# Hybrid decoder trunk: forget logits by row products on VectorE, the first weight block in four pieces, and two operations moved ahead of the last eviction

## What is computed

```python
def token_mixer_block(x, w_in, ...):
    h = jnp.einsum('bsd,dn->bsn', x, w_in)          # n = 10 * 512 + 4
    (p_in, hq, hf, hi, hg, gu, gv, fq, fk, fv, ff) = jnp.split(h, splits, axis=-1)
    ...
    d = fox_mixer(fq, fk, fv, ff + b_fox_f)
    ...
    gates = jax.nn.sigmoid(jnp.einsum('bsd,dn->bsn', x, w_gate) + b_gate)

def reference(x, ...):
    for l in range(DEPTH):
        x = layer_norm(ALPHA * x + token_mixer_block(...), ln1_g[l], ln1_b[l])
        x = layer_norm(ALPHA * x + peer_ffn(...), ln2_g[l], ln2_b[l])
```

## Time and profile before

| | us |
|---|---|
| median of 3 runs | 3813.95 (3813.29 to 3815.09) |
| the profiled execution's own time | 3812.06 |
| its span, from first to last instruction | 3810.1 |
| TensorE matmul busy | 3728.1 (98% of the span) |
| VectorE busy | 2730.8 (72%) |
| ScalarE busy | 1487.8 (39%) |
| mean granted TensorE clock | 0.996 of full |

### The profile page before, as it was taken

The page is one execution under the profiler, slowest core; times in us unless marked ns, Lnnn a source line. Parts: engine busy times, 40 slices in busy tenths (PEclk is TensorE's granted clock), DMA queues, the critical chain, the costliest instruction groups (busy, mean ns, idle before and its releaser), DMA issues. The chain is left out here.

```text
span 3810.1 us, 53339 instructions
## 1 busy us (share of the span) xinstructions
PE 3728.1 (98%) x19506; PEld 3310.0 (87%) x19506; DVE 2730.8 (72%) x5347; ACT 1487.8 (39%) x2154; POOL 1284.5 (34%) x1040
## 2 busy tenths in 40 slices
PE   8999999999999999999999999999999999999998
PEld 7878888999999999988878788889999899999887
DVE  3257635499989888878642566355999888888887
ACT  2244522244763333333322445223447533333332
POOL 1000000265856555544000000002658556555440
PEclk9999999999999999999999999999999999999999
DMA  4212423254689999999732225233537899999995
GB/s 148 101 56 75 161 91 138 108 184 157 216 287 382 358 355 348 344 346 354 257 133 94 65 68 171 78 139 112 206 142 229 302 378 357 358 350 344 342 357 208
DMA packets 321524, 847.59 MB, mean 222 GB/s; under 512 B 21056, under 2 KB 119360, under 8 KB 296256
## 3 DMA queue, kind: packets, MB, share of 16 engines
q1 hardware_dynamic: 247616, 576.84, 42.9%
q0 software_dynamic: 73728, 268.47, 18.8%
HBM read 755.58 MB, written 89.65 MB: 222 GB/s over the span
## 5 line engine op out<-in xcount | busy, mean ns | idle before, releaser
L93 PE MATMUL bank<-xT_low,u_high 128*128 128x384 f32 (+1 forms) x2144 | 728.9, 340 | 11.5 <-ACT hid L1897 7.3
L95 PE MATMUL bank<-xT_high,u_low 128*128 128x384 f32 (+1 forms) x2144 | 723.4, 337 | 0.0
L94 PE MATMUL bank<-xT_high,u_high 128*128 128x384 f32 (+1 forms) x2144 | 723.1, 337 | 0.0
L93 PE MATMUL bank<-v_low,w_high 128*128 128x512 f32 x1536 | 597.7, 389 | 0.9 <-DVE v_low L1998 0.9
L95 PE MATMUL bank<-v_high,w_low 128*128 128x512 f32 x1536 | 598.2, 389 | 0.0
L94 PE MATMUL bank<-v_high,w_high 128*128 128x512 f32 x1536 | 598.1, 389 | 0.0
L1189 POOL TENSOR_TENSOR u_low<-merged,u_high 128x1024 fp32r<-128x1024 f32 x96 | 243.1, 2546 | 1043.8 <-ACT u_high L1184 1043.6
L1257 POOL DMA_INDIRECT far_rows<-peer_v_dram,far_index x256 | 389.3, 1521 | 415.3 <-DVE x_far L1281 369.5
L1257 POOL DMA_INDIRECT far_rows<-peer_u_rows_dram,far_index x256 | 374.8, 1464 | 312.6 <-DVE far_dots L1263 259.7
L1998 DVE TENSOR_TENSOR v_low<-v_raw,v_high 128x1024 fp32r<-128x1024 f32 x256 | 301.8, 1221 | 207.4 <-ACT v_high L1909 207.3
L1909 ACT ACTIVATE v_high<-v_raw 128x1024 fp32r<-128x1024 f32 x256 | 257.3, 1052 | 472.2 <-PE bank L95 467.2
(11 more groups left out here) (445 smaller groups left out, 6811.3 us busy)
## 6 DMA issues: line engine op xcount, KB each, us to landing
merged<-peer_u_dram SPq DMA_DIRECT2D x128, 1024.0 KB, 7.7
v_raw<-peer_v_dram SPq DMA_DIRECT2D x128, 1024.0 KB, 9.4
gates_scratch<-stage SPq DMA_DIRECT2D x24, 2048.0 KB, 8.3
G<-gates_scratch SPq DMA_DIRECT2D x64, 768.0 KB
hidden_scratch<-ahead_hid SPq DMA_DIRECT2D x60, 384.0 KB, 2.6
hid<-hidden_scratch SPq DMA_DIRECT2D x30, 768.0 KB, 7.1
mg_raw<-w_merge_dram SPq DMA_DIRECT2D x28, 768.0 KB, 4.3
first_raw<-w_in_dram SPq DMA_DIRECT2D x20, 1024.0 KB, 5.6
```

Of the source, the lines that this page charges most:

```text
L93: nc.tensor.matmul(out, lh, rl, start=first, stop=False)
L94: nc.tensor.matmul(out, lh, rh, start=False, stop=False)
L95: return nc.tensor.matmul(out, ll, rh, start=False, stop=last)
```

## The change

1. **Forget logits.** w_ff is loaded as four rows of 1024, broadcast to all 128 partitions, into projN[:, 2:4], which is free until the last pair. VectorE makes 16 products with sum (`tensor_tensor_reduce`, 128x1024: each of 4 tiles with each of 4 rows), after the low part of pair 1's block 1 (and the constants) and ahead of all evictions of pair 1; ScalarE waits for all 16 before its first eviction of pair 1. The 24 matmuls, w_ff's splits and their buffers are gone; TensorE transposes the 4 tiles of sums, 128x4 each, into bank 0, ahead of bank 7 of the last pair.
2. **First weight block.** In the first layer, block 0 is loaded and split in four pieces of two k each. VectorE's order: piece 0, tile 0 of x, pieces 1 to 3. TensorE waits for each piece in `first(0, 0)`. `first(t, 0)` runs for all four tiles, then `first(t, 1)`; `turn(t+1)` is issued in the middle of `first(t, 0)`. So block 0's buffer is free halfway through pair 0, and pair 1's block 0 is split there.
3. **The end.** VectorE's copy to ffT and gate block 0's low part come ahead of its last eviction (bank 7).

```diff
+                dots = sb(ctx, "in_dots", [P, NT, WT])
+                w_ff = projN[:, 2:4].rearrange("p b t n -> p (b t n)").rearrange("p (h d) -> p h d", d=D_MODEL)
+                products = [early[:, D_MODEL * i:D_MODEL * (i + 1)] for i in (8, 9)]
...
+                            load_tokens(0)
+                            for r in range(2):
+                                for half, landed in enumerate((first_in[r], loaded[r])):
+                                    sp.dma_start(quarter(raw, r, half), a["w_in"][layer, block_of(0, 0)][:, 4 * r + 2 * half:4 * r + 2 * half + 2, :]
+                                                 ).then_inc(landed, 16)
+                            for t in range(1, NT):
+                                load_tokens(t)
...
-                        sp.dma_start(w_ff[:], a["w_ff"][layer]).then_inc(small_in, 16)
+                        sp.dma_start(w_ff, a["w_ff"][layer].partition_broadcast(P)).then_inc(ff_in, 16)
...
+                        sp.wait_ge(ff_dots, WT)
                         load_next(sp)
...
+                                if layer == 0 and b == 0 and k == 4 and t + 1 < NT:
+                                    turn(t + 1)
...
+                        def turn_dots():
+                            pe.wait_ge(ff_dots, NT * WT)
+                            pe.wait_ge(kept[0], 4 * n_pairs - 3)
+                            for t in range(NT):
+                                tr = nc.tensor.transpose(bank[0][0:WT, t * P:(t + 1) * P], dots[:, t, :], ident[:])
+                            tr.then_inc(ff_turned, 1)
...
+                                    if token_major and n == 7:
+                                        turn_dots()
...
-                        pe.wait_ge(small_l, 1)
-                        pe.wait_ge(kept[0], 4 * n_pairs - 3)
-                        for k in range(KT):
-                            mm = matmul_split(nc, bank[0][0:WT, :], (sh[:, k, :], sl[:, k, :]), (xh[:, k, :], xl[:, k, :]),
-                                              k == 0, k == KT - 1)
-                        mm.then_inc(mm_done, 1)
...
+                        act.wait_ge(ff_dots, NT * WT)
                         pairs_after_first(act, high, copy, scaled, 0)
...
+                        dve.wait_ge(ff_in, 16)
+                        for t in range(NT):
+                            for h in range(WT):
+                                if t or h > 1:
+                                    dve.wait_ge(ff_dots, WT * t + h - 1)
+                                nc.vector.tensor_tensor_reduce(out=products[h % 2], in0=norm.tokens(t), in1=w_ff[:, h, :], scale=1.0, scalar=0.0,
+                                                               op0=ALU.mult, op1=ALU.add,
+                                                               accum_out=dots[:, t, h:h + 1]).then_inc(ff_dots, 1)
+                        dve.wait_ge(ff_dots, NT * WT)
+                        def before_last():
+                            dve.wait_ge(ff_turned, 1)
+                            nc.vector.tensor_copy(ffT[:], bank[0][0:WT, :])
+                            dve.wait_ge(gate0_high, 1)
+                            nc.vector.tensor_tensor(gate0[1], gate0_raw, as_f32(gate0[0]), ALU.subtract).then_inc(gate0_low, 1)
+                        pairs_after_first(dve, low, copy, scaled, 1, before_last)
```

More of the change, by code:

```diff
@@ L431, in _ @@
                             turn(0)
-                        for t in range(NT):
-                            first(t, 0)
-                            if layer and t == 0:
-                                first(t, 1)
-                            if t + 1 < NT:
-                                turn(t + 1)
-                            if layer == 0 or t:
-                                first(t, 1)
+                            for b in range(2):
+                                for t in range(NT):
+                                    first(t, b)
+                        else:
+                            for t in range(NT):
+                                first(t, 0)
+                                if t == 0:
+                                    first(t, 1)
+                                if t + 1 < NT:
+                                    turn(t + 1)
+                                if t:
+                                    first(t, 1)
                         with pe.Fori(1, n_T + 1) as j:
@@ L491, in high, with high_quarter @@
                                 nc.scalar.activation(wh[b][:, 4 * r:4 * r + 4, :], raw[:, r], ACT.Copy).then_inc(w_high, 1)
-                        for t in range(NT):
-                            if layer and t:
-                                norm.root(act, t)
-                            if t < 2 and layer == 0:
-                                high(0, t)
-                            elif t == 0:
-                                high(0, 1)
-                            if layer == 0 or t:
+                        def high_quarter(r, half):
+                            act.wait_ge(loaded[r] if half else first_in[r], 16)
+                            nc.scalar.activation(quarter(wh[0], r, half), quarter(raw, r, half), ACT.Copy
+                                                 ).then_inc(w_high if half else first_high, 1)
+                        if layer == 0:
+                            high_quarter(0, 0)
+                            norm.high(act, 0)
+                            high_quarter(0, 1)
+                            high_quarter(1, 0)
+                            high_quarter(1, 1)
+                            norm.high(act, 1)
+                            norm.high(act, 2)
+                            high(0, 1)
+                            keep_first(act, copy, 0, 0)
+                            norm.high(act, 3)
+                            for t in range(1, NT - 1):
+                                keep_first(act, copy, 0, t)
+                        else:
+                            high(0, 1)
+                            for t in range(1, NT):
+                                norm.root(act, t)
                                 norm.high(act, t)
-                            if t:
                                 keep_first(act, copy, 0, t - 1)
@@ L788, in build_program @@
                         with ExitStack() as c2:
-                            w_ff = sb(c2, "w_ff", [P, KT, WT], side="right")
                             def load_gate(sp):
```

76 lines of the change are left out of this document (45 added, 31 removed).

## The result

| | before | changed |
|---|---|---|
| median of the runs taken side by side, us | 3814.77 (3813.29 to 3815.09, 5 runs) | 3792.73 (3791.45 to 3794.36, 5 runs) |
| the profiled execution's own time / span, us | 3812.06 / 3810.1 | 3791.45 / 3789.7 |
| TensorE matmuls | 19506 | 19466 |

The account below looks back on a forecast made before the run. TensorE, busy 98% of the span, bounds the kernel. Gains of 5.5 (start) + 6.2 + 6.2 (stage ends) = 17.9 us take 3812.06 to 3794.2, or 3796.0 against the median 3813.95; range 3792.5 to 3801.5.

Parts of the forecast that it names:

- First matmul at 8.9: Start of the first layer: TensorE's first matmul on first_low at 8.9 us instead of 14.40, 5.5 us earlier.
- halfway, at 5.9: Start of the first layer: the first 512 KB of weights land at 5.9 us, halfway through the first megabyte's 2.29 us.
- Pair 0 takes 49.12 us: First layer: pair 0 takes as long as before (14.40 to 63.52), so pair 1 begins at 58.0.
- a term of 5.5: Start of the first layer: loading and splitting the first weight block in pieces gains 5.5 us.
- Fed through pair 0: First layer, pair 0: pieces 1 to 3 are ready a microsecond or more before TensorE wants them, so no wait.
- Products 1.15 us apart: VectorE during pair 1: 16 products take 18.4 us in each layer, from 68.8 in the first, at no cost.
- room 8.7 and 7.7: Pair 2's first low half is ready 8.7 us (first layer) and 7.7 us (second) before TensorE wants it.
- Rival C: Pair 2's first matmul, both layers: the products outlast pair 1 and TensorE waits; 3824 us, chance 0.03.
- Stage end 6.2 in each layer: End of the stage: TensorE resumes at 239.2 instead of 245.39, 6.2 us earlier, and 6.2 again in the second layer.
- Rival A: Start of the first layer: pieces load one after another, losing 3.8 us; 3805 us, chance 0.11 together with smaller losses.
- Rival B: End of the stage: the clock falls after the idle stretch, losing 1.6 to 2.75 us each; 3799 to 3801.5, chance 0.10.
- the forecast's own range: Whole kernel: 3794 to 3798.5 us around 3796.0, for slow pace at the start, transposes and late pieces; chance 0.76.

Follow-up runs that it names:

- e4: Changed kernel with block 0 still in four pieces but pair 0 in the old order; 3801.02 us, ratio 0.9972 to the kernel before.
- e3: Changed kernel with VectorE's copy to ffT and the gate block's low part behind its last eviction; 3795.59 us, ratio 0.9957 to the kernel before.
- e7: Changed kernel with the first weight block in two halves of 4 k; 3797.16 us, ratio 0.9959 to the kernel before.
- e6: Changed kernel with the first weight block in five pieces of 1, 1, 2, 2, 2 k; 3792.73 us, ratio 0.995 to the kernel before.
- e10: Changed kernel with 8 more products behind the 16 in each layer; 3795.33 us, ratio 0.9955 to the kernel before.
- e8: Changed kernel with 16 more products behind the 16 in each layer; 3818.26 us, ratio 1.0019 to the kernel before.

## Why the prediction held, and where it was off

- **First matmul at 8.9: 9.27.** The step that was off is the landing: "halfway, at 5.9" was 6.3. ScalarE's 1.05 and VectorE's 1.14 were right (1.06, and 1.17 to the next operation).
- **Pair 0 takes 49.12 us: 48.08 and 48.58.** That figure was one execution's; before's second profile has 48.21. Two of each kernel give 63.14 and 57.60 for pair 1: 5.54 us, for a term of 5.5. That it meets the term so closely is luck: the first matmul gained 5.2 us in the mean, and the other 0.3 come from the number of slow matmuls, which differs by 3 to 4 between executions of one program. The forecast named 1.1 us of uncertainty here, and the runs show 0.2 us a slow matmul.
- **Fed through pair 0: yes**, but for a reason that the prediction gave in half a sentence. e4 shows that without the new order a wait of 4.00 us for block 1 takes the whole gain. The working checked pieces 1 to 3 and tile 1, and not the load behind them; it came out right because the order was part of the change, and not because the sum had seen it.
- **Products 1.15 us apart, from 68.8, room 8.7 and 7.7:** 1.146 apart, from 68.04, room 9.0 and 7.8. Rival C needed 1.63 us a product.
- **Stage end 6.2 in each layer:** 6.10 in the first and 6.11 in the second, on two profiles of each kernel. From the last eviction to the mixer it is 7.60 before and 1.02 now; the four transposes delay that eviction by 0.47 us, where the sum had 0.40. e3 splits it.
- **Rival A (pieces in turn):** refuted; 1.3 us a piece, no wait in pair 0. With halves of 1 MiB (e7) the first matmul is 2.75 us later, and two first pieces of 256 KB (e6) gain nothing, so the best size seen lies between. The Trainium skill, "DMA: Bandwidth & Descriptors", section Bandwidth, advises DMAs of at least 1 MiB; at this place the trace disagrees: 512 KB in 1.3 us is not much slower than the 2.29 us of the megabyte before, and what the stage waits for is the first piece alone.
- **Rival B (clock at the stage end):** it did not happen behind the wait of 1.06 us: the granted clock is 1.00 from 233.12 to 240, and from the mixer's first matmul to the first group of L2248 it is 3.71 us, before (L2181) 3.73. But the prediction argued it from the first matmul's 0.47 us, and that row proves little: e3 has the same 0.47 behind a wait of 2.77 us, and then slows and loses 1.6 us, the lower end of the rival's price. The change escapes Rival B because part 3 keeps the wait short.
- **The sum:** 17.9 forecast, 22.0 by medians, 21.4 and 19.8 by ratios. The terms of the edited stages came out at 5.54 + 6.10 + 6.11, that is 17.8. No stage shows a term that the forecast missed, and one execution differs from another by some 3 us either way, nearly the whole difference. That the total met the range is in part luck: 3792.73 lies 0.2 us inside its lower end and below the forecast's own range of 3794 to 3798.5, and the second set of runs has 3791.08.

## What to carry to other kernels

Splitting a first load pays only if the order of the consumer gives the next load time to come: look at what is wanted 24 matmuls later, not at the piece alone. Work moved to an engine with slack is free up to a room that can be read from the trace (ready against wanted) and was exact to 0.3 us here; beyond it TensorE waits for the rest, and a wait of 9 to 11 us cost 2 us more by the slow pace behind it. To see whether a wait slows TensorE, read on past the first matmul behind it. When two profiles of one program differ by 6 us, compare distances inside the edited stage, not spans.

## What the runs showed that I had not expected

- The last slow matmul at the start of the first layer begins between 12.4 and 14.1 us for kernels that start at 9.3, and at 16.2 in e6, which starts at 7.55 and stands still in between. Transposes of the identity matrix in TensorE's idle time, 12 from 1.60 us on and 16 behind tile 0's, remove the slow pace: 1.8 us earlier at pair 1 in the profile, not seen in the totals.
- The pace can fall some time after a wait and not at once. Behind 1.06 us (stage end) and 1.36 us (e10) it stayed fast. Behind 2.77 us (e3) it fell 1.24 us after TensorE had resumed, in the second layer 0.53 us after, and behind 4.00 us (e4) 1.51 us after; behind 9.34 us (e8) it was slow from the first matmul.
- TensorE's waits in the experts' first part add up to 1.9 or 6.7 us in two executions of the same kernel. Their cause was not looked for.
